# Mixer of a two-block transformer kernel: order of the sums of activations, the modulation pieces and their loads

## The reference

```python
mods = jnp.split(jax.nn.silu(c) @ w_ada[l] + b_ada[l], N_MOD, axis=-1)
sh1, sc1, gt1, sh2, sc2, gt2, sh3, sc3, gt3 = mods
...
u = modulate(rmsnorm(h, g_mix[l]), sh2, sc2)
proj = u @ w_in[l]
qa, ka, va, xm, o_pre, ga, gb = jnp.split(proj, split_idx, axis=-1)
...
merged = jax.nn.sigmoid(ga) * (ya @ w_proj_a[l]) + jax.nn.sigmoid(gb) * (yb @ w_proj_b[l])
h = h + gt2[:, None, :] * (merged @ w_out[l])
u = modulate(rmsnorm(h, g_ff2[l]), sh3, sc3)
```

## Time and profile before

| what | value |
|---|---|
| median of 3 runs | 1180.81 us (1180.71 to 1181.24) |
| the profiled execution | 1179.22 us, its span 1177.4 us |
| TensorE busy | 1164.3 us, 99% of the span |
| VectorE busy | 737.2 us, 63% |
| ScalarE busy | 352.1 us, 30% |
| GpSimd busy | 86.2 us, 7% |
| granted TensorE clock, mean | 0.997 |

### The profile page before, as it was taken

The page is one execution under the profiler, slowest core; times in us unless marked ns, Lnnn a source line. Parts: engine busy times, 40 slices in busy tenths (PEclk is TensorE's granted clock), DMA queues, the critical chain, the costliest instruction groups (busy, mean ns, idle before and its releaser), DMA issues.

```text
span 1177.4 us, 21319 instructions
## 1 busy us (share of the span) xinstructions
PE 1164.3 (99%) x8862; PEld 1076.8 (91%) x8862; DVE 737.2 (63%) x1658; ACT 352.1 (30%) x996; POOL 86.2 (7%) x104
## 2 busy tenths in 40 slices
PE   9999999999999999999999999999999999999997
PEld 7889999998878999999999999988888998888887
DVE  4558888675148866982898888567845231167632
ACT  2111210232124555212321210245333431056542
POOL 0000000200011000022000000310004010001111
PEclk9999999999999999999999999999999999999999
DMA  9969949762655457676599759574524643642311
GB/s 344 366 217 321 315 154 313 290 245 90 219 180 187 150 214 259 236 264 231 185 342 304 235 201 294 193 260 171 146 61 144 215 144 114 187 136 73 117 63 36
DMA packets 164272, 241.78 MB, mean 205 GB/s; under 512 B 14033, under 2 KB 112559, under 8 KB 164176
## 3 DMA queue, kind: packets, MB, share of 16 engines
q1 hardware_dynamic: 156256, 230.45, 57.9%
q10 hardware_dynamic: 6784, 5.74, 1.7%
q0 software_dynamic: 1136, 4.22, 1.1%
HBM read 236.82 MB, written 4.62 MB: 205 GB/s over the span
## 4 chain that ended last, share of the span: by engine, by line
PE 91%; DVE 5%; DMA 2%; ACT 1%; issue 1%; POOL 0%; DVEq 0%; ACTq 0%
PE ps L189 89%; PE ps L192 2%; DVE arena L198 2%; DMA slots<-in_w_proj_a 1%; DVE x L198 1%; DMA slots<-in_w_proj_b 1%; ACT U L195 1%; DVE slots L207 1%; ACT tmps L195 0%; DVE arena L204 0%; DVE rstd L216 0%; DVE tmps L204 0%; DVE slots L198 0%; DVE tmps L198 0%; POOL arena L198 0%
## 5 line engine op out<-in xcount | busy, mean ns | idle before, releaser
L189 PE MATMUL ps<-U,slots 128*128 128x128 f32 (+2 forms) x2800 | 478.7, 330 | 0.0
L189 PEld LDWEIGHTS ps<-U,slots 128*128 128x128 f32 (+1 forms) x2800 | 419.7, 190 | 40.7 <-issue 4.7
L189 PE MATMUL ps<-arena,slots 128*128 128x128 f32 (+1 forms) x1776 | 237.6, 294 | 0.0
L189 PEld LDWEIGHTS ps<-arena,slots 128*128 128x128 f32 x1776 | 225.3, 192 | 8.6 <-issue 0.4
L195 ACT ACTIVATE tmps<-ps 128x256 f32<-128x256 f32 (+2 forms) x151 | 57.4, 383 | 343.4 <-PE ps L189 319.4
L207 DVE CUSTOM_DVE_ANT_0 arena<-arena,tmpA 128x1024 f32<-128x1024 f32 x96 | 118.2, 1275 | 19.3 <-DMA arena<-in_w_adaT 19.1
L195 ACT ACTIVATE arena<-ps 128x256 f32<-128x256 f32 (+3 forms) x150 | 59.5, 416 | 155.9 <-PE ps L189 152.1
L189 PE MATMUL ps<-arena 128*128 128x128 f32 (+7 forms) x940 | 101.9, 287 | 0.9 <-DVE arena L198 0.9
L189 PEld LDWEIGHTS ps<-arena 128*128 128x128 f32 (+2 forms) x940 | 92.4, 181 | 9.8 <-issue 4.2
L189 PE MATMUL ps<-ABT,arena 128*128 128x128 f32 (+5 forms) x752 | 81.9, 271 | 0.0
L189 PEld LDWEIGHTS ps<-ABT,arena 128*128 128x128 f32 (+3 forms) x752 | 72.5, 174 | 0.8 <-issue 0.8
(11 more groups left out here) (199 smaller groups left out, 1140.6 us busy)
## 6 DMA issues: line engine op xcount, KB each, us to landing
slots<-in_w_in SPq DMA_DIRECT2D x14, 2048.0 KB, 10.3
slots<-in_w_down SPq DMA_DIRECT2D x16, 1408.0 KB, 9.8
slots<-in_w_gate SPq DMA_DIRECT2D x18, 1024.0 KB, 8.0
slots<-in_w_up SPq DMA_DIRECT2D x18, 1024.0 KB, 10.8
arena<-in_w_adaT SPq DMA_DIRECT2D x36, 512.0 KB, 6.1
arena<-in_ada_w1T SPq DMA_DIRECT2D x24, 512.0 KB, 7.5
slots<-in_a_in_w SPq DMA_DIRECT2D x6, 2048.0 KB, 9.8
slots<-in_b_in_w SPq DMA_DIRECT2D x12, 1024.0 KB, 5.4
```

The source lines that it names most:

```text
L189: return Nothing() if self.e is None else self.e.matmul(*a, **k)
```

## The change

Four edits, all in the order of work; no operation is added or removed.

1. `sync`: in each of the five groups the modulation block is fetched after the two weight blocks instead of before them.
2. `vector`: at j = 28 and 32, where the source changes, `v_t7_3` of ("pa", 0) and ("pb", 0) comes after `v_s7`. Before, it stood at j = 27 and 31, ahead of the piece of that step.
3. `vector`: a table `PIECES` says which of the pieces 0 to 15 each j does: none at 14 to 17, one each at 18 to 23, two each at 24, 25, 26, none at 27, one each at 28 and 29, two at 30. The bias sums of blocks 13, 14, 15 come at j = 22, 25, 28, that of block 16 behind the loop.
4. `vector`: pieces 16 to 19 (block 17) come after the residuals of pairs 0 and 1 of `wo`, two each, and the bias sum of block 17 after the last residual of that loop.

```diff
                 fetch("k", b)
             for n, g in (("ga", 13), ("gb", 14), ("op", 15), ("pa", 16), ("pb", 17)):
-                fetch("ada", g)
                 fetch(n, 0)
                 fetch(n, 1)
+                fetch("ada", g)
...
+        PIECES = {18: (0, 1), 19: (1, 2), 20: (2, 3), 21: (3, 4), 22: (4, 5), 23: (5, 6), 24: (6, 8), 25: (8, 10), 26: (10, 12),
+                  28: (12, 13), 29: (13, 14), 30: (14, 16)}
...
                     if j == 32:
                         v_s7(e, "hc", HC, [dve.at("yb", k) for k in range(8)], ("pa", 1))
+                    if j in (28, 32):
+                        v_t7_3(e, U7.index(("pa" if j == 28 else "pb", 0)))
                     v_u7_c1(e, i)
...
                         if j != 3:
                             v_t7_12(e, i + 1)
-                        v_t7_3(e, i + 1)
+                        if j not in (27, 31):
+                            v_t7_3(e, i + 1)
...
-                if j >= 18 and j % 4 == 2 and j < 35:
-                    v_ada_mods(e, 13 + (j - 18) // 4)
-                if 14 <= j < 34:
-                    v_ada_blocks(e, 13, 2 * (j - 14), 2 * (j - 14) + 2)
+                n0, n1 = PIECES.get(j, (0, 0))
+                if n0 and n0 % 4 == 0:
+                    v_ada_mods(e, 12 + n0 // 4)
+                v_ada_blocks(e, 13, 2 * n0, 2 * n1)
+            v_ada_mods(e, 16)
             v_gated_b(e, 1, 1)
...
             for pair in range(4):
                 v_residual(e, "wo", pair, sm[:, 128:136], "n2", 0 if pair >= 2 else None)
+                if pair < 2:
+                    v_ada_blocks(e, 13, 32 + 4 * pair, 36 + 4 * pair)
+            v_ada_mods(e, 17)
             v_scale(e, "n3", V("g_ff2"), 56)
```

## The result

The changed kernel takes a median of 1183.09 us over 12 runs, the kernel before 1181.17 us over 12 runs beside it. The ratio is 1.0018, 95% interval [1.001, 1.0025]: +2.1 us, where the forecast was +0.8, inside the range (1179.6 to 1183.6). It is a change of 0.2%, and its interval lies clear of none. One execution of each kernel took far longer (2438.6 and 1986.3 us) and is left out of the ratio.

What follows compares the result with a forecast made beforehand. TensorE, busy 99% of the span, was taken as the bound, so only its gaps counted. Mixer -1.2 plus n3 sums +2.0 gave +0.8 us: 1180.0 profiled, 1181.6 us as median (1.6 above the profiled execution), range 1179.6 to 1183.6.

Steps and rivals of the forecast that it cites:

- The mixer: Stretch up to the out-projection: both waits for sums of activations go, one new gap comes; net -1.2 us.
- a new gap at p7 of ("op", 1): TensorE in the mixer waits there for ScalarE's late normalisation and copy u2; 1.0 us.
- the tanh chain behind c22: ScalarE in the mixer: two more pieces delay VectorE's c22, so tanh, table load, normalisations and u2 come 1.03 us later.
- At ("pb", 0): Second new-source block in the mixer: sums of activations come in time, removing TensorE's loss of 0.78 us.
- GpSimd's queue behind bias sum 17: After the out-projection's residuals, n3's sums of squares stand behind this wait and a load, delaying TensorE; +2.0 us.
- The hold of the DMA, the unknown of the sum: GpSimd's load ahead of n3's sums of squares: taken as 0.57 us; no hold gives +1.4, upper end +11.
- The term of the sums of n3: TensorE starts n3's norm sums at 553.5 instead of 551.58: 1.9 us, plus 0.1 for the refill, +2.0 us.
- The load of ("ada", 16): Mixer weight load: lands at 482.8, 0.4 us before its first piece, with 0.6 more before ("pb", 0) feels it; no cost.
- The first, that the queue doesn't bite: n3's sums of squares are ready in time, leaving only the mixer's gain: 1179.6, or 1178.5 without the new gap; 8%.
- The second, that GpSimd is held by its DMA: Between bias sum 17 and the first sum of squares, each microsecond beyond 0.57 costs TensorE one; 2 more: 1183.6; 12%.
- The third, that the mixer gives nothing: ("ada", 16) lands late or the tanh chain is longer, so the mixer's gain is lost: 1182.8, at worst 1183.5; 18%.
- The +0.2 us: Mixer's sum if a table-switch drain made the chain behind the late tanh 1.4 us longer: -1.2 + 1.4; not used.

Runs made afterwards that it cites:

- the respread pieces: Changed kernel with GpSimd's sums of squares of n3 ahead of its wait, and no two pieces at any step from 16 to 29: 1178.8 us, ratio 0.9982.
- the version with the squares first: Changed kernel with GpSimd's sums of squares of n3 ahead of its wait for bias sum 17 and its load: 1180.03 us, ratio 0.9986.
- the version with the wait first and the load last: Changed kernel with GpSimd's conditioning vector load behind the sums of squares of n3, the wait for bias sum 17 ahead of both: 1181.65 us, ratio 1.0003.
- late wait in the old one: Kernel before, with GpSimd also waiting for VectorE's scale of n3 ahead of its load and sums of squares: 1184.43 us, ratio 1.0023.
- two repeated sums: Changed kernel with GpSimd's load behind the sums of squares of n3 and one 128x128 sum among them repeated twice, result unused: 1183.31 us, ratio 1.002.

## Why the prediction was right, and where it was short

**Right, with its sizes.** The mixer: -1.27 us, predicted -1.2. Its two parts: a new gap at p7 of ("op", 1) of 1.01 us (1.0 predicted), and a net -0.48 us at ("pa", 0) (-0.4); the tanh chain behind c22 is shown by the respread pieces, which take the gap away. At ("pb", 0) -0.79 more (-0.78). The place and the cause of the loss: GpSimd's queue behind bias sum 17, shown by the version with the squares first. The hold of the DMA, the unknown of the sum, was taken as 0.57 us: the first sum starts at 550.44, 0.59 us behind the issue at 549.85. The end of the issue was right, its start was not, as the next paragraph says.

**The term of the sums of n3** was +2.0 us, 1.9 for the start and 0.1 behind it, and measured 2.27 and 0.10. The hand-over from VectorE to GpSimd was sized too small: the bias sum ends at 549.52 and the issue starts at 549.85, 0.33 us, where I had 0.07. With a sum in the place of the issue the 0.07 would have been right: it is 0.08 in the version with the wait first and the load last.

**The step that failed** is the sentence that puts the cost of the wait at its length and 0.1 for the refill, and says that nothing downstream takes it back. Both halves are wrong. The wait costs what it lasts and 0.1, and then 1.63 us more at the 1.2 GHz level; and the next wait, of 0.35 us at the second sums, is taken in by the shift and gives 0.62 us back. That is +1.01 us of the 1.3 that lie between +0.8 and +2.1; the hand-over with the rest of its term is 0.37, less 0.07 from the mixer. No row ahead of the prediction that I had set out for the sum bore on the clock after such a gap: the longest of its rows has an idle time of 1.23 us, which, like 1.72 us here, costs little beyond itself. But the trace of the kernel before does show the half level, at 8 to 11 us of the span, and the prediction drew nothing from it. I took the granted clock of 0.997 as a mean and asked of no term whether it could change it. It was a missing case with a price, and would have moved the forecast to 1181.6 + 1.0 = 1182.6. That the measured 1183.09 lies inside the range is in part luck: its upper end stood where it did for a longer hold of the DMA, not for the clock.

**The one that was nearly short.** The load of ("ada", 16) was to land 0.4 us before its first piece. VectorE's timeline has it late by 0.23:

```profile
485.23 1.23 DVE L207 CUSTOM_DVE_ANT_0 slots<-slots,tmpA 128x1024 f32<-128x1024 f32 x1 [0.23 <-DMA slots<-in_w_adaT]
```

It cost nothing, as the 0.6 us behind it held: no wait for `x` stands at ("pb", 0).

**The rivals.** The first, that the queue doesn't bite, counted five sums of squares where six have to fit in, and fell with the wait of 2.08 us; its time of 1179.6 is about what the squares first give (0.9986 x 1181.17 = 1179.5). The second, that GpSimd is held by its DMA, fell with the 0.59 us, but for the 0.25 us ahead of the issue: the time went 1.5 us past the forecast towards its 1183.6, but by another mechanism. The Trainium skill, "Perfetto Trace Analysis", DMA Instruction — SWDGE, says that the slice on this engine ends when the last descriptor is written; the row fits that, with the next sum 0.02 us behind the slice's end. That the issue also starts 0.25 us later than a sum would is not in the slice. The third, that the mixer gives nothing, fell with the mixer's -1.27. And where I set the measured table load against the drain of 1380 ns that the Trainium skill, "ScalarE: Activation LUTs", What ACT_TABLE_LOAD costs, adds at each switch, the trace of the changed kernel has again none: the load at 467.32 ends at 468.60, and the normalisations start at 468.73, behind a root that stands between. The +0.2 us that I drew from it would not have followed anyway, for a drain would stand in the rows of the kernel before as well and not lengthen the chain between the two.

## What to carry to other kernels

When a bias sum or any small result moves later, look up who waits for it, and what stands behind that wait in the same queue: four edits that won 1.3 us on VectorE lost 3.4 us on GpSimd, and moving one line won it all back. Price a new gap of the matrix engine by its length, and then look at the granted clock behind it: at one place of this kernel 0.5 us more of gap cost 1.63 us more of half clock, while the two gaps that were removed from the mixer (1.23 and 0.53 us) had cost 0.26 and 0.25 us beyond themselves. Look for stretches at the lower level in the trace that you have, before you take a mean of 0.997 as none. Work that fills room must go where the step has room: the same pieces, one to a step instead of two at steps 24 to 26, kept the whole 2.26 us.

## What was not expected of the hardware

- The granted clock fell to half after an idle stretch of 2.08, 2.09 and 2.19 us at the same place of the program (changed kernel, late wait in the old one, two repeated sums), fell within 1.1 us of TensorE's return and stayed low for over 3 us; after 1.23 and 1.72 us it stayed at 1.00. The half pair behind it lasted 5.36 or 5.37 us in all three, against 3.74. Near the start of the kernel before it fell after an idle time of only 0.58 us.
- That half clock came with the DMA engines full (share 1.09) and idle (0.00) alike.
- The issue of a DMA by GpSimd took 0.84 us out of its chain, 0.25 of them ahead of the row of 0.57 (changed kernel against the version with the load last).
- The profiled executions come in two patterns at their start, whatever the kernel: the mixer's first transposes start at 356.42 to 356.46 in four of them (the kernel before among them) and at 358.31 to 359.01 in six others. In the four early ones the granted clock is at half from about 7.6 to 11 us, in the others it is not. Two spans of single profiles differ by that without a cause in the code, so stretches are to be compared from a common row on.
